# Operand addresses at 128 modulo 256 and column halves in the row-stationary matmuls of a two-block layer stack

## What is computed

```python
proj = rms_norm(x) @ w_in            # ssm: 1024 x 2048, attention: 1024 x 4096
y = y * sigmoid(y @ w_glu + b_glu);  h = h + (y * silu(z)) @ w_out
...
h = rms_norm_2(x); proj = h @ w_in[l]      # latent 416, conv 1024, retention 3072, gates 3072 columns
y_mla, y_conv, y_ret = mla(...) @ w_o, conv(...) @ w_pw, retention(...) @ w_o
x = x + rms_norm_2((g0*y_mla + g1*y_conv + g2*y_ret) @ w_out[l])
f = (silu(h @ ffn_w_gate[l]) * (h @ ffn_w_up[l])) @ ffn_w_down[l];  x = x + rms_norm_2(f)
```

## Time and profile before

| what | value |
|---|---|
| three runs, median | 1236.93 us (1235.34 to 1237.02) |
| the profiled execution | 1237.6 us |
| its span, first to last instruction | 1235.8 us |
| mean granted TensorE clock | 0.995 of full |
| TensorE busy with matmuls | 1205.2 us, 98% |
| TensorE busy with weight loads | 1013.5 us, 82% |
| VectorE, ScalarE, GpSimd busy | 73%, 52%, 8% |
| moved by DMA | 215.68 MB, mean 175 GB/s |

### The profile page before, as it was taken

How to read it: one execution, slowest core, us unless ns; L and a number is a source line. 1 busy time by engine, 2 the same in 40 slices (tenths; PEclk the granted TensorE clock), 3 DMA queues, 4 the chain that set the end, 5 groups by cost and what they waited for, 6 DMA issues and landing times.

```text
span 1235.8 us, 19035 instructions
## 1 busy us (share of the span) xinstructions
PE 1205.2 (98%) x7597; PEld 1013.5 (82%) x7597; DVE 901.5 (73%) x1463; ACT 639.1 (52%) x1034; POOL 100.4 (8%) x163
## 2 busy tenths in 40 slices
PE   7999999999999999999999999999999999999998
PEld 3566778888988788787999987988788787999986
DVE  7998877757589998687666655589997687665553
ACT  4334565665556665545444544556575545444441
POOL 6300011101000200201000001000200201000000
PEclk9999999999999999999999999999999999999999
DMA  7635666434565555354766664565445355565552
GB/s 251 221 94 173 205 208 191 156 119 146 163 205 168 155 157 187 133 169 164 216 201 188 193 195 154 174 211 169 158 153 188 132 170 170 190 197 193 191 194 75
DMA packets 71958, 215.68 MB, mean 175 GB/s; under 512 B 16256, under 2 KB 19744, under 8 KB 71744
## 3 DMA queue, kind: packets, MB, share of 16 engines
q1 hardware_dynamic: 65008, 206.37, 52.0%
q0 software_dynamic: 2112, 6.97, 1.8%
q10 hardware_dynamic: 4752, 1.14, 0.4%
HBM read 208.95 MB, written 3.15 MB: 172 GB/s over the span
## 4 chain that ended last, share of the span: by engine, by line
PE 86%; DVE 8%; ACT 3%; issue 2%; POOL 1%; DMA 0%; DVEq 0%; POOLq 0%; ACTq 0%
PE acc L700 17%; PE acc L702 17%; PE acc L701 17%; PE acc L678 7%; PE acc L680 7%; PE acc L679 7%; PE acc L639 3%; PE mixed L1015 1%; DVE weights_lo L1776 1%; PE mixed L1112 1%; ACT junk L1279 1%; PE turned L755 1%; DVE h_T L1806 1%; PE mixed L999 1%; PE mixed L1008 1%
## 5 line engine op out<-in xcount | busy, mean ns | idle before, releaser
L1776 DVE TENSOR_TENSOR weights_lo<-weights_raw,weights_hi 128x1024 fp32r<-128x1024 f32 (+1 forms) x304 | 355.7, 1204 | 71.6 <-ACT weights_hi L1244 71.0
L1244 ACT ACTIVATE weights_hi<-weights_raw 128x1024 fp32r<-128x1024 f32 (+1 forms) x304 | 305.8, 1043 | 80.8 <-DMA weights_raw<-stream_dram 80.6
L700 PE MATMUL acc<-weights_hi,act_F_hi 128*128 128x512 f32 (+1 forms) x680 | 275.7, 406 | 5.6 <-DVE act_F_lo L1806 3.4
L702 PE MATMUL acc<-weights_hi,act_F_lo 128*128 128x512 f32 (+1 forms) x680 | 267.2, 393 | 0.0
L701 PE MATMUL acc<-weights_lo,act_F_hi 128*128 128x512 f32 (+1 forms) x680 | 265.4, 390 | 0.0
L678 PE MATMUL acc<-act_F_hi,weights_hi 128*128 128x256 f32 x624 | 173.6, 278 | 0.0
L679 PE MATMUL acc<-act_F_hi,weights_lo 128*128 128x256 f32 x624 | 172.5, 276 | 0.0
L680 PE MATMUL acc<-act_F_lo,weights_hi 128*128 128x256 f32 x624 | 172.4, 276 | 0.0
L700 PEld LDWEIGHTS acc<-weights_hi,act_F_hi 128*128 128x128 f32 x680 | 128.7, 189 | 34.2 <-DVE act_F_lo L1806 4.3
L702 PEld LDWEIGHTS acc<-weights_hi,act_F_lo 128*128 128x128 f32 x680 | 128.4, 189 | 28.4
L701 PEld LDWEIGHTS acc<-weights_lo,act_F_hi 128*128 128x128 f32 x680 | 128.7, 189 | 25.6
(11 more groups left out here) (339 smaller groups left out, 1923.6 us busy)
## 6 DMA issues: line engine op xcount, KB each, us to landing
weights_raw<-stream_dram SPq DMA_DIRECT2D x306, 512.0 KB, 3.7
weights_raw_more<-stream_dram SPq DMA_DIRECT2D x58, 512.0 KB, 4.3
gains<-rows_dram POOLq DMA_DIRECT2D x12, 512.0 KB, 4.8
weights_raw<-stream_dram SPq DMA_DIRECT2D x6, 416.0 KB, 3.1
weights_raw<-stream_dram SPq DMA_DIRECT2D x4, 384.0 KB, 3.5
x_T<-x_in_dram SPq DMA_DIRECT2D x4, 256.0 KB, 6.0
ssm_bc<-ssm_bc_dram SPq DMA_DIRECT2D x1, 1024.0 KB, 8.6
u_scratch<-u_T ACTq DMA_DIRECT2D x4, 256.0 KB, 5.5
```

The lines of the kernel that those rows point to most:

```text
L700: pe.matmul(o, xh, wh, start=first and kk == 0, stop=False)
L702: i = pe.matmul(o, xl, wh, start=False, stop=last and kk == s["nk"] - 1)
L1244: act.activation(high(s, slice(0, n)), whole(s, slice(0, n)), ACT.Copy).then_inc(hi_made, 1)
L1776: dve.tensor_tensor(low(s, slice(0, n)), whole(s, slice(0, n)), high(s, slice(0, n)).bitcast(F32), ALU.subtract).then_inc(lo_made, 1)
```

## The change

The weights move from 192 to 128 modulo 256 (`weights_offset` goes), `act_F` stays where it was because `rows_offset` grows by the same 64 bytes, `mla_F` moves from 0 to 128 with a wider `latent_rows_offset`, `conv_F` stays at 128, and the filler `mla_heads` is widened so that the two extra places come to 128 as well. In `tile_slot` each product of width `w` is made as two of `w // 2` columns: first the three matmuls of the left half, then the three of the right half, with a load of the stationary tile for each. The flag that clears the bank stands on the very first matmul only. A half of 512 columns is 1024 bytes, so the right half begins at 128 modulo 256 too; half of 416 is 208 columns (832 bytes), half of 384 is 192 (768 bytes).

```diff
-        sb("weights_offset", [P, 16])
...
-        sb("rows_offset", [P, 16])
+        sb("rows_offset", [P, 32])
...
-            sb("latent_rows_offset", [P, 24], F32, s4)
+            sb("latent_rows_offset", [P, 56], F32, s4)
...
-                sb("conv_rows_offset", [P, 24], F32, s6)
+                sb("conv_rows_offset", [P, 56], F32, s6)
...
-                sb("mla_heads", [P, 3880], F32, s6)
+                sb("mla_heads", [P, 3896], F32, s6)
...
                 for kk in range(s["nk"]):
                     k = k0 + s["k"] + kk
-                    wh, wl = (f(at, slice(kk * w, (kk + 1) * w)) for f in (high, low))
                     xh, xl = (f[:, k, t * P:(t + 1) * P] for f in (hi, lo))
-                    o = acc[par][t][:, 0:w]
-                    pe.matmul(o, xh, wh, start=first and kk == 0, stop=False)
-                    pe.matmul(o, xh, wl, start=False, stop=False)
-                    i = pe.matmul(o, xl, wh, start=False, stop=last and kk == s["nk"] - 1)
+                    ends = last and kk == s["nk"] - 1
+                    for half in range(2):
+                        a, b = half * w // 2, (half + 1) * w // 2
+                        wh, wl = (f(at, slice(kk * w + a, kk * w + b)) for f in (high, low))
+                        o = acc[par][t][:, a:b]
+                        pe.matmul(o, xh, wh, start=first and kk == 0 and half == 0, stop=False, skip_group_check=True)
+                        pe.matmul(o, xh, wl, start=False, stop=False, skip_group_check=True)
+                        i = pe.matmul(o, xl, wh, start=False, stop=ends, skip_group_check=True)
                 return i
```

## The result

The changed kernel takes **1281.86 us** (median of four runs, 1281.39 to 1281.99) against 1236.97 us for the kernel before in the same comparison: a ratio of 1.0361, 95% interval 1.0349 to 1.0374. It is 45 us slower. I had predicted 1235.7 us, range 1203 to 1252.

What follows compares the result with a forecast made beforehand. TensorE, busy 98% of the span, was taken as the bound; 7.2 us less for halved 512s, 6.0 more for narrow halves and 0 for moved weights gave 1.2 us less, 1235.7 us for the median, range 1203 to 1252.

Steps and rivals of the forecast that it cites:

- Part 1: Halving the 2952 row-stationary products of 512 columns: 676.3 us now, 669.1 us after at 113.33 ns a half, 7.2 us less.
- The 5 ns of mla_F's products: The 120 products of 512 columns with rows in mla_F take 234 ns against 228.9, adding 0.6 us to today's cost.
- Part 3: Moving weights from 192 to 128 leaves the 2496 weight-stationary matmuls and the streams of the halves at 113.33 ns: 0 us.
- The upper bound I gave, 117 ns: Highest distance allowed per matmul with weights at 128, from four 16-column matmuls; the lower bound was 106.7 ns.
- Part 2: Halving the row-stationary products of 416 and 384 columns: 26.6 us becomes 32.6 us, 6.0 us more (3.9 to 7.1).
- the slope of the loads' durations: Loads take 189 ns for 128 columns, 109 for 32: 0.83 ns a column, about 107 ns for a full load.
- The break-even of 113.5 ns: Time per row-stationary half above which halving loses: 702.9 us over 6192 halves; each nanosecond on it is worth 6.2 us.
- Rival (b): Row-stationary stretches: loads become the bound, halves at 116 ns, 1252 us; chance 0.22, all slower.
- (a): Halves and weight-stationary matmuls: streams and loads both starting at 128 hinder each other less, 110 ns each, 1207 us; chance 0.28.
- both unknown distances: Start-to-start times of the row-stationary halves and of weight-stationary matmuls with weights at 128, each taken as 113.33 ns.

## Why the prediction was wrong

**The reading of the bottleneck held.** TensorE alone sets the time, clock and feeding did not change, and the 45 us are longer steps of its own.

**Part 1, "the nearest row is the weight-stationary stretch ... at 113.33", is the larger step that failed.** I had the halved 512s at 7.2 us less; by the usual steps, 120.0 ns a half, they are 32.2 more. The value is real: halves do run at 113.3 in three kernels. But the row I took it from had stream and load 64 bytes apart, and the change puts them at the same place. I had both addresses and did not ask whether the price belonged to the shape or to the pair of addresses. The 5 ns of mla_F's products had shown that addresses count. Even 64 bytes apart the price was not safe: most trains of halves ran at 118 there, and the halved 512s took 4.8 us more where 7.2 less were forecast.

**Part 3, "Weights from 192 to 128 ... 0 us", failed for the same reason.** It cost 16.7 us. I rested it on one hand-over, where a tile at 128 was loaded under a stream at 128 and took 0.12 us. Two starts read to 0.01 us cannot tell 113 from 120, and it was a single load of that kind in a train of loads at 192; 863 in a row take 120.1 ns. The upper bound I gave, 117 ns, came from fp32 groups and did not hold the value either.

**Part 2 held.** The narrow halves take 111.5 and 111.3 ns, I took 113.3 with 106 and 117 as ends; they cost 5.5 us where I said 6.0. That 208 and 192 columns take the same agrees with its reading that the load sets the distance there; the slope of the loads' durations gave 107 ns for one, 4 too few.

**The break-even of 113.5 ns held and decides the case.** No train that was seen gave a 256-column matmul below 113.3 ns, so two halves never beat 226.7, and a whole product at equal starts takes just that with one load instead of two.

**Rival (b)** had the sign and the place, loads that fill the row-stationary stretches, at 116 ns; (a), alignment as a gain, has the opposite sign. But (b)'s mechanism is only half of it: loads alone don't make 120 ns, since the weight-stationary stretch was as full before at 113.3. In the row-stationary stretches it takes a full train of loads *and* equal starts: halves 64 bytes apart run at 113 to 118, whole products at equal starts at 226.8. The Trainium skill's "TensorE: Matmul & The Clock Gate", section "Back-to-back issue gap", had the sign of the halving by a fixed cost per matmul, in a formula that it gives for a matmul by itself. These runs do not bear its size out, as two halves at 113.3 take less than one whole at 228.9. The section "Operand start alignment" of "SBUF — State Buffer" in the Trainium skill has no price for a start; here 64 bytes are worth 6.7 ns in 113.

The range missed because I let both unknown distances end at 116 to 117 ns, and priced the high one for the halves alone, never for halves and weight-stationary matmuls together.

## What to carry to other kernels

Before a price is taken over from a stretch of the same shape, list what else that stretch has fixed, here the two start addresses, and ask whether the change moves it. A single hand-over is no measurement of a steady stream, and one stretch is none of all stretches: look for the same instructions elsewhere in the trace, as in the attention here. For fp32r operands as in this kernel, 64 bytes between stream and load were the best place tried where a stationary tile is loaded under every stream of 256 columns, though in its slow rhythm, at 117.8 ns, it is no better than 32 bytes, at 116.7 and 118.4. Where one load lies under a stream of 512 columns, equal starts gave the shortest distances. Cutting such a product in two cost time both at equal starts and at the old places; there it took 4.8 us for the products of 512 columns.

## What the runs showed of the hardware

- The cost of an fp32r matmul of 256 columns with its own load depends on where the streamed and the loaded operand start relative to each other: 113.4 ns at 64 bytes in its better rhythm, 116.7 to 120.1 at the other distances, 120.0 at equal starts whether both are at 128 or at 192, and 120.0 again at 256 bytes. Why is not shown.
- At 64 bytes a train has two rhythms, 113.3 and 117.8 ns. It keeps the one it starts with, for some 860 matmuls at most here, and the same instructions can have either; what decides is not shown.
- For narrower streams this vanishes: halves of 192 columns took 111.3 ns at equal starts and 111.2 at 64 bytes (halving alone, 5.23 us over 47 steps in both). Halves of 208 columns, whose streams start at 128, 192, 0 and 64 in turn over loads at 128, took 111.5.
- The shortest seen in trains are 113.3 ns for 256 columns and 226.7 for 512. Both are 0.443 ns a column, which at the granted 2.4 GHz is 17/16 of a cycle.
